# Tables of angles for the state space branch: sums of turns and ScalarE sines in the place of powers by doubling

## The chip, the cores and the metric

The kernel runs on one core of a Trainium2 chip. Its time is the device time of one execution in microseconds (us); the figure compared is the median of several runs. One further execution was taken by the hardware profiler; every row below comes from it.

## What is computed

The reference runs two layers of a hybrid block (Mamba-2, sliding-window and forgetting attention) over 256 tokens of width 1024, then one layer of a second block. That block normalizes the tokens, projects them, and adds three branches: a diagonal state space branch (S5), a sparse attention that keeps 64 keys per query, and attention over a memory. After that comes a mixture of experts, two of 32 per token. The change touches the state space branch alone:

```python
def s5_branch(u, lam_re, lam_im, log_dt, b_re, b_im, c_re, c_im, d_skip, w_glu):
    ...
    lam = lax.complex(lam_re.astype(F32), lam_im.astype(F32))
    dt = jnp.exp(log_dt.astype(F32))[:, None]
    lam_bar = jnp.exp(lam * dt)
    b = lax.complex(b_re.astype(F32), b_im.astype(F32))
    b_bar = ((lam_bar - 1.0) / lam)[..., None] * b
    bu = jnp.einsum('bsgh,gph->bsgp', uf.astype(jnp.complex64), b_bar)
    a = jnp.broadcast_to(lam_bar, (1, seq) + lam_bar.shape)
    _, states = lax.associative_scan(_ssm_combine, (a, bu), axis=1)
    ...
```

There are 32 groups of 64 states, 2048 complex states in all, held as 16 columns of 128 partitions. The recurrence h[n] = lam_bar h[n-1] + bu[n] is turned into two real ones: with lam_bar = rad * e^(i th), the inputs are turned back by n*th, run through a real scan with the factor rad, and turned forward by n*th. For this the kernel needs cos(n*th) and sin(n*th) for n = 0 to 255 and all 16 columns of states: two tables of 128 x 4096 numbers.

## The kernel before

The five engines each run a program of their own, written by hand, and meet at semaphores. A stage is a list of matrix products, each cut into pieces of weights; `weave` and `braid` fix by tables of counts after how many pieces a step of side work comes. Every engine goes through the same list, so the order on an engine never changes at run time, and an engine that waits at one step holds all that stands behind it.

The stages around the change, in the order in which they run:

- `last` of the second layer: TensorE multiplies with weights split in halves (ScalarE casts the high half, `w_hi`, line 2057; VectorE subtracts, `w_lo`, line 1154). Woven in is `prepare` (VectorE from line 1530, ScalarE from 2280): decay `rad` and angle `th` for each state, the rotary angles, and the norm of the memory. In `prepare` VectorE also squares the 16 numbers c5 + i s5 seven times over (`wc`, `ws`), giving the powers 1, 2, 4 ... 128 of e^(i th).
- `kmv`: TensorE projects the memory with whole weights (line 680). Beside it ScalarE and VectorE normalize the tokens (`normalize`), and VectorE then waits for TensorE's transposes and copies them out (`do_split`, the tile `h_all`).
- `table()` on VectorE: the tables for the first 8 columns of states (`R[0]` cosines, `R[2]` sines) by doubling. Entry m+j is entry j times the power m; eight rounds, from 8 x 1 to 8 x 128 columns. GpSimd does the same for the other 8 columns (`R[1]`, `R[3]`), once VectorE is done (`tables_made`) and after the scaling of two quarters of the output matrices (`scale_quarter`, lines 2492 to 2501). VectorE waits for it at unit 4 (`table_made`).
- `u`: TensorE's projection of the branch's inputs, 4 pieces.
- `side`: the 32 steps of `BRAID`. S steps are the state space branch. TensorE's first transposes `uT` and makes `inputs(0)` (line 956); its step for unit u makes `inputs(u+1)`, and for even u from 2 on `outputs` (line 965) before that. VectorE's `unit(u)` turns the inputs, scans them and turns the states, and frees the two PSUM banks of `inputs(u)`, which `inputs(u+1)` takes again. C steps are the sparse attention: its head on VectorE (norm, rotation), transposes, scores (line 917), the search for the 64 highest, then attention. M steps are the memory attention. After each step come 0 to 4 pieces of the projections. The braid begins

```python
BRAID = [("S", 4), ("S", 2), ("S", 2), ("C", 4), ("S", 2), ("C", 0), ("C", 3), ("S", 3), ("C", 3), ("S", 2), ("C", 0), ("C", 1), ("C", 0),
```

so VectorE runs unit 0, unit 1, the head of the sparse attention, unit 2, the first search, unit 3 and so on, in that order.

## Time and profile before

| | |
|---|---|
| median of 3 runs | 2177.31 us (2173.54 to 2178.78) |
| profiled execution | 2178.17 us, of which 2176.3 us are the span between its first and last instruction |
| TensorE matmuls | busy 2006.9 us, 92% of the span |
| VectorE | 1526.8 us, 70% |
| ScalarE | 1117.2 us, 51% |
| GpSimd | 135.6 us, 6% |
| chain that ended last | TensorE 70%, VectorE 20%, ScalarE 5% |

A matmul's busy time overlaps that of its neighbours, so 92% does not mean that TensorE was never kept waiting; the waits are read from its own timeline. Times in the rows are from the start of the span.

### The profile page before, as it was taken

How to read it: one execution, taken by the hardware profiler on the slowest of the kernel's cores; microseconds unless marked ns; L12 is line 12 of the kernel's file. 1: busy time of each engine (PE TensorE's matmuls, PEld its weight loads, DVE VectorE, ACT ScalarE, POOL GpSimd, SP SyncE). 2: the span in 40 equal slices, each digit the busy share in tenths (PEclk: the TensorE clock that was granted, in tenths of full speed). 3: DMA queues.
4: the chain of work that ended last, by engine and by line, in shares of the span. 5: the costliest groups of instructions: out<-in, count | busy, mean ns of one | idle time of the engine just before them, and what ended most of it. 6: DMA issues, size and time to landing. Idle time of an engine off the chain costs nothing.

```text
span 2176.3 us, 25594 instructions
## 1 busy us (share of the span) xinstructions
PE 2006.9 (92%) x9470; PEld 1557.7 (72%) x9470; DVE 1526.8 (70%) x2283; ACT 1117.2 (51%) x1679; POOL 135.6 (6%) x139
## 2 busy tenths in 40 slices
PE   7898999999988899998986889879999999999996
PEld 6777777777877677776543445547888888888885
DVE  5868565555776755557398855338888888888885
ACT  5544554444543555444301022037777777778773
POOL 0000000000000000000074110010000000000000
PEclk9999999999999999999998889989999999999998
DMA  7533434354543444444342322346999999999993
GB/s 227 160 117 117 135 117 136 100 154 147 175 154 88 146 117 126 117 148 153 114 144 83 116 87 97 105 178 236 330 337 329 329 329 324 342 324 330 328 327 136
DMA packets 135325, 411.15 MB, mean 189 GB/s; under 512 B 17789, under 2 KB 19581, under 8 KB 108065
## 3 DMA queue, kind: packets, MB, share of 16 engines
q1 hardware_dynamic: 128912, 407.25, 56.2%
q0 software_dynamic: 6288, 2.26, 0.4%
q8 instruction: 76, 1.25, 0.2%
q14 instruction: 49, 0.39, 0.1%
HBM read 406.23 MB, written 19.47 MB: 196 GB/s over the span
## 4 chain that ended last, share of the span: by engine, by line
PE 70%; DVE 20%; ACT 5%; issue 3%; DMA 1%; SPq 0%; DVEq 0%; ACTq 0%; POOLq 0%
PE bank L632 16%; PE bank L633 16%; PE bank L634 16%; PE bank L680 7%; DVE r L1154 5%; PE bank L1040 3%; DVE w_lo L1154 3%; PE bank L608 2%; PE bank L754 2%; DVE r L1160 1%; ACT w_hi L2057 1%; DVE small L1154 1%; DVE spare L1154 1%; PE bank L803 1%; ACT r L2232 1%
## 5 line engine op out<-in xcount | busy, mean ns | idle before, releaser
L1154 DVE TENSOR_TENSOR w_lo<-w_raw,w_hi 128x1024 fp32r<-128x1024 f32 x372 | 445.3, 1217 | 230.8 <-ACT w_hi L2057 223.3
L2057 ACT CAST w_hi<-w_raw 128x1024 fp32r<-128x1024 f32 x266 | 277.2, 1047 | 166.3 <-PE bank L634 160.0
L632 PE MATMUL bank<-w_hi,h_hi 128*128 128x512 f32 x800 | 329.7, 412 | 18.7 <-DVE w_lo L1154 18.7
L633 PE MATMUL bank<-w_lo,h_hi 128*128 128x512 f32 x800 | 316.7, 396 | 0.0
L634 PE MATMUL bank<-w_hi,h_lo 128*128 128x512 f32 x800 | 316.5, 396 | 0.0
L632 PEld LDWEIGHTS bank<-w_hi,h_hi 128*128 128x128 f32 x800 | 153.5, 192 | 55.7 <-DVE w_lo L1154 13.8
L634 PEld LDWEIGHTS bank<-w_hi,h_lo 128*128 128x128 f32 x800 | 153.1, 191 | 34.2
L633 PEld LDWEIGHTS bank<-w_lo,h_hi 128*128 128x128 f32 x800 | 154.0, 193 | 29.5
L2232 ACT ACTIVATE r<-bank,small 128x256 f32<-128x256 f32 (+1 forms) x152 | 63.8, 424 | 202.4 <-DVE small L1157 202.4
L1154 DVE TENSOR_TENSOR w_lo<-r,w_hi 128x1024 fp32r<-128x1024 f32 x106 | 126.4, 1222 | 30.9 <-ACT w_hi L2342 30.9
L680 PE MATMUL bank<-w_raw,h_all 128*128 128x512 f32 (+1 forms) x320 | 146.1, 613 | 1.1 <-DVE h_all L1154 1.1
L2342 ACT CAST w_hi<-w_raw 128x1024 fp32r<-128x1024 f32 x106 | 109.9, 1056 | 18.7 <-PE bank L634 18.6
L680 PEld LDWEIGHTS bank<-w_raw,h_all 128*128 128x128 f32 x320 | 63.7, 201 | 74.7 <-issue 72.5
L2342 ACT CAST w_hi<-r 128x1024 fp32r<-128x1024 f32 x106 | 109.9, 1060 | 5.2 <-PE bank L634 5.2
L632 PE MATMUL bank<-w_hi,xt_hi 128*128 128x512 f32 x280 | 112.0, 400 | 0.0
L633 PE MATMUL bank<-w_lo,xt_hi 128*128 128x512 f32 x280 | 110.1, 393 | 0.0
L634 PE MATMUL bank<-w_hi,xt_lo 128*128 128x512 f32 x280 | 110.1, 393 | 0.0
L632 PE MATMUL bank<-w_hi,y_hi 128*128 128x512 f32 x256 | 102.9, 402 | 4.9 <-DVE y_lo L1154 3.0
L634 PE MATMUL bank<-w_hi,y_lo 128*128 128x512 f32 x256 | 100.5, 393 | 0.0
L633 PE MATMUL bank<-w_lo,y_hi 128*128 128x512 f32 x256 | 100.5, 393 | 0.0
L1154 DVE TENSOR_TENSOR y_lo<-r,y_hi 128x1024 fp32r<-128x1024 f32 x70 | 84.8, 1224 | 9.3 <-ACT y_hi L2342 8.8
L1438 DVE TENSOR_REDUCE small<-bank 128x2 f32<-128x512 f32 (+1 forms) x76 | 43.8, 576 | 59.1 <-PE bank L928 28.8
(341 smaller groups left out, 4038.7 us busy)
## 6 DMA issues: line engine op xcount, KB each, us to landing
w_raw<-in_w_in SPq DMA_DIRECT2D x236, 512.0 KB, 3.7
r<-in_w_up SPq DMA_DIRECT2D x69, 1024.0 KB, 5.4
w_raw<-in_w_gate SPq DMA_DIRECT2D x68, 1024.0 KB, 5.1
w_raw<-in_w_down SPq DMA_DIRECT2D x36, 1024.0 KB, 5.2
r<-in_w_down SPq DMA_DIRECT2D x34, 1024.0 KB, 5.2
w_raw<-in_w_proj SPq DMA_DIRECT2D x48, 512.0 KB, 3.7
w_raw<-in_w_out SPq DMA_DIRECT2D x24, 512.0 KB, 4.4
w_raw<-in_w_mem_kv SPq DMA_DIRECT2D x8, 512.0 KB, 3.5
```

Source lines behind the costliest of these rows:

```text
L608: done = e.transpose(bank[0:blk.shape[1], j * P:(j + 1) * P], blk, ident)
L632: e.matmul(out_, sh, mh, start=first, stop=False, skip_group_check=shared)
L633: e.matmul(out_, sh, ml, start=False, stop=False, skip_group_check=shared)
L634: return e.matmul(out_, sl, mh, start=False, stop=last, skip_group_check=shared)
L680: done = e.matmul(bank[:, 0:c.n], c.lhs[0][:, kk, t * P:(t + 1) * P], w[:, k, :], start=kk == 0, stop=kk == c.n_k - 1)
L754: done = e.matmul(banks[b][:, c:c + dv], pT[:, (j * kb + kk) * P:(j * kb + kk + 1) * P], v_of(h, kk), start=(kk == 0), stop=(kk == kb - 1))
L1040: done = e.matmul(bank[:, j * 256:(j + 1) * 256], ht[half][:, t, (2 * i + j) * P:(2 * i + j + 1) * P], slots[q % 2][:, t, :, :], start=t = ...
L1154: o.did(v.tensor_tensor(out_, a, b, op), sem, value)
L1438: o.did(v.tensor_reduce(mx, two[:, :, 0:keys_of(t)], AX, MAX))
L2057: a.copy(halves(n)[0], raw_of(n)).then_inc(w_hi, 1)
L2232: a.activation(p_buf[i % 2][:, j * keys:(j + 1) * keys], bank[:, 0:keys], ACT.Exp, bias=mx_all[:, c + j:c + j + 1], accum_out=sum_all[:, c ...
L2342: a.copy(unit_halves(u)[0], unit_raw(u)).then_inc(m_hi, 1)
```

## The change

The 16 columns of states are now cut into two halves of 8 by `table(0)` and `table(1)`, as before, but the entries are no longer products. `turns()` on VectorE expresses the angle as a share of a whole turn (`thn`), takes the whole turns off by adding and subtracting a constant that rounds (`ROUND`), and makes two small tables of 16 numbers for each state: a16 = 0, 16, ... 240 steps and b1 = 0, 1, ... 15 steps. `table(half)` on VectorE adds them, 8 x 16 x 16 = 2048 sums per partition, and takes the whole turns off again. `table(half)` on ScalarE makes the cosine as the sine of a quarter turn less the absolute angle, and the sine. VectorE waits for the first half at unit 0 and for the second at unit 4. The seven squarings in `prepare` go, and GpSimd makes no table; it scales its four quarters one after the other, as their matrices land.

On VectorE `turns()` and `table(0)` stand ahead of `do_split`, `table(1)` behind it. On ScalarE `table(0)` stands behind `kmv`, and `table(1)` between the two evictions of `u`, by `weave(dense(e2["u"]), table(1), n_pieces(e2["u"]), [2], 2)`. The diff without the declarations of semaphores and the removed bodies in full:

```diff
@@ -332,7 +332,7 @@
         ang, sn2, cs2, tmp2, n2 = (stat(64) for _ in range(5))
         sn3, cs3 = tok(sn2), tok(cs2)
         dt5, rad, th, thn, tht, c5, s5, nr, ni, fr5, fi5, den = (stat(ST) for _ in range(12))
-        wc, ws = [c5] + [stat(ST) for _ in range(7)], [s5] + [stat(ST) for _ in range(7)]
+        quarter_turn = stat(1)
         at[0] += -at[0] % 8
         inverse = over_tile("inverse", S, "small", at[0])[0:3, :]
         head_stats, mem_stats = ([stat(T * n) for _ in range(3)] for n in (9, 8))
@@ -1552,13 +1552,6 @@
                     o.prev()
                     tt(dst, dst, den, MUL)
                 o.prev()
-                for j in range(7):
-                    tt(wc[j + 1], wc[j], wc[j], MUL)
-                    tt(tht, ws[j], ws[j], MUL)
-                    o.prev()
-                    tt(wc[j + 1], wc[j + 1], tht, SUB)
-                    stt(ws[j + 1], wc[j], 2.0, ws[j], MUL, MUL)
-                    o.prev()
                 yield
                 v.wait_ge(in_pos, 32)
                 o.did(v.tensor_copy(pos_f[:, :], R[10][:, 0:T + S].bitcast(I32)))
@@ -1577,25 +1570,43 @@
                     tt(memT[:, k:k + 4, t * P:(t + 1) * P], by_k(bank[:, :], 4), bc(small_cols[:, COLS2["g_mem"] + k:COLS2["g_mem"] + k + 4], P), MUL, drained[b], n)
                 yield
 
-            def table():
-
-                ec, es = by_k(R[0][:, :], 8), by_k(R[2][:, :], 8)
-                t1, t2 = (by_k(R[8][:, i * D:(i + 1) * D], 8) for i in range(2))
...
+            def turns():
+
+                first = by_k(R[8][:, 0:512], 2 * ST)
+                whole = by_k(R[8][:, 512:1024], 2 * ST)
+                o.did(v.memset(quarter_turn, HALF_PI))
+                ts(thn, th, TURNS, None, MUL)
+                o.prev()
+                ts(tht, thn, 16.0, ROUND, MUL, ADD)
+                o.prev()
+                ts(tht, tht, ROUND, None, SUB)
+                o.prev()
+                stt(tht, thn, 16.0, tht, MUL, SUB)
+                steps = index_row[:, 0:16].unsqueeze(1).to_broadcast([P, ST, 16])
+                tt(first[:, ST:2 * ST, :], steps, bc(thn, 16), MUL)
+                o.prev()
+                tt(first[:, 0:ST, :], steps, bc(tht, 16), MUL)
+                o.prev()
+                ts(whole, first, ROUND, None, ADD)
+                o.prev()
+                stt(first, whole, ROUND, first, SUB, SUB)
+                o.prev()
+
+            def table(half):
+
+                a16, b1 = (by_k(R[8][:, 0:512], 2 * ST)[:, i * ST + 8 * half:i * ST + 8 * half + 8, :] for i in range(2))
+                turn, whole = (R[i + half][:, :] for i in (2, 0))
+                for i in range(2):
+                    part = slice(4 * i, 4 * i + 4)
+                    tt(turn[:, i * D:(i + 1) * D].rearrange("p (s a b) -> p s a b", s=4, a=16), a16[:, part, :].unsqueeze(3).to_broadcast([P, 4, 16, 16]),
+                       b1[:, part, :].unsqueeze(2).to_broadcast([P, 4, 16, 16]), ADD)
+                o.prev()
+                for i in range(2):
+                    ts(whole[:, i * D:(i + 1) * D], turn[:, i * D:(i + 1) * D], ROUND, None, ADD)
+                o.prev()
+                for i in range(2):
+                    cols = slice(i * D, (i + 1) * D)
+                    stt(turn[:, cols], whole[:, cols], ROUND, turn[:, cols], SUB, SUB, turns_made)
 
             def by_h(a, h):
                 return a.rearrange("p (h c) -> p h c", h=h)
@@ -1719,8 +1730,8 @@
                     ec, es = (a[:, sl, :] for a in angle(k))
                     vre, vim = (by_k(a, 4)[:, sl, :] for a in v_at[k % 2])
                     tm, gr, gi = tmp[:, sl, :], gre[:, sl, :], gim[:, sl, :]
-                    if u == 4:
-                        v.wait_ge(table_made, 1)
+                    if u in (0, 4):
+                        v.wait_ge(table_made, 2 + u // 2)
                     (b0, n0, bank0), (b1, n1, bank1) = await_full(("bu", k, j2, 0)), await_full(("bu", k, j2, 1))
                     bre, bim = by_k(bank0[:, :], 2), by_k(bank1[:, :], 2)
                     o.prev()
@@ -2022,9 +2033,11 @@
             for t in range(T):
                 stt(x3[:, t, :], x3[:, t, :], r[:, t:t + 1], R[9][:, 0:D], MUL, MUL, scaled_made)
             normalize(x3, normed2)
+            turns()
+            table(0)
             run(dense(e2["kmv"]))
             do_split(e2["h"])
-            table()
+            table(1)
             run(dense(e2["u"]))
             braid(dense(e2["side"]), S=ssm(), C=sparse(), M=memory())
             run(dense(e2["memory"]))
@@ -2289,6 +2302,15 @@
                 a.wait_ge(in_mem, 32)
                 rms_factor(mem3, normed)
                 yield
+                yield
+
+            def table(half):
+                sine, cosine = R[2 + half][:, :], R[half][:, :]
+                a.wait_ge(turns_made, 2 * half + 2)
+                a.activation(cosine, sine, ACT.Abs).then_inc(turned_abs, 1)
+                a.wait_ge(turned_abs, half + 1)
+                a.activation(cosine, cosine, ACT.Sin, bias=quarter_turn, scale=-2 * PI).then_inc(table_made, 1)
+                a.activation(sine, sine, ACT.Sin, scale=2 * PI).then_inc(table_made, 1)
                 yield
 
             def sparse():
@@ -2459,8 +2481,9 @@
             a.wait_ge(scaled_made, T)
             rms_factor(x3, normed2)
             run(dense(e2["kmv"]))
+            run(table(0))
             do_split(e2["h"])
-            run(dense(e2["u"]))
+            weave(dense(e2["u"]), table(1), n_pieces(e2["u"]), [2], 2)
             braid(dense(e2["side"]), S=ssm(), C=sparse(), M=memory())
             run(dense(e2["memory"]))
             weave(dense(e2["last"]), bridge(), n_pieces(e2["last"]), BRIDGE)
@@ -2501,33 +2524,9 @@
                 o.did(g.tensor_scalar(c1, c1, -1.0, None, MUL), quarter_scaled)
                 o.prev()
 
-            def table():
-
...
             def ssm():
                 g.wait_ge(bias_used, sum(c.bias is not None for e in L for c in e["forget"] + e["last"]))
-                for k in range(2):
-                    scale_quarter(k)
-                table()
-                for k in range(2, 4):
+                for k in range(4):
                     scale_quarter(k)
 
             def store_rows(x):
```

On VectorE, behind the norm of the tokens and ahead of the copies `h_all` of their transposes, where the rows with + are new (in `small` lie the angles, in the `r` tiles the turns and tables):

```order
 L1157 TENSOR_SCALAR r<-x,small 128x1024 x2
+L1577 MEMSET small 128x1
+L1157 TENSOR_SCALAR small<-small 128x16 x3
+L1160 SCALAR_TENSOR_TENSOR small<-small 128x16
+L1154 TENSOR_TENSOR r<-consts,small 128x256 x2
+L1157 TENSOR_SCALAR r<-r 128x512
+L1160 SCALAR_TENSOR_TENSOR r<-r 128x512
+L1154 TENSOR_TENSOR r<-r 128x1024 x2
+L1157 TENSOR_SCALAR r<-r 128x1024 x2
+L1160 SCALAR_TENSOR_TENSOR r<-r 128x1024 x2
 L1154 TENSOR_TENSOR h_all<-bank,small_cols 128x4x128 x4
```

Nine new rows with 15 instructions now stand between the norm and the copies. On VectorE again, between those copies (`h_all`) and the first operation of unit 0 (`spare_52<-bank,r`), the last rounds of the old table and all of the new one:

```order
-L1154 TENSOR_TENSOR r<-r,small 128x8x128
-L1154 TENSOR_TENSOR r<-r,small 128x1024
-L1154 TENSOR_TENSOR r<-r,small 128x8x128
-L1154 TENSOR_TENSOR r<-r,small 128x1024
-L1154 TENSOR_TENSOR r<-r 128x8x128 x2
+L1154 TENSOR_TENSOR r<-r 128x1024 x2
+L1157 TENSOR_SCALAR r<-r 128x1024 x2
+L1160 SCALAR_TENSOR_TENSOR r<-r 128x1024 x2
 L1154 TENSOR_TENSOR spare_52<-bank,r 128x512
```

The whole doubling, from 128x8 on, is gone from this place, and six instructions of 1024 columns stand there. On ScalarE, from the last evictions of `kmv` (COPY r<-bank) on, through those of `u`, to the copies of `uT` (`spare_51<-bank`) and the evictions of `q2` and `kvi`, before:

```order
L2063 ACTIVATE small<-small 128x2
L2117 COPY r<-bank 128x512 x6
L2172 COPY spare_51<-bank 128x4x128 x2
L2117 COPY r<-bank 128x512 x2
L2117 COPY r<-bank 128x452 x2
L2061 ACT_TABLE_LOAD
L2061 ACTIVATE small<-small 128x18
```

and with the change:

```order
L2130 COPY r<-bank 128x512 x4
L2310 ACTIVATE r<-r 128x2048
L2312 ACT_TABLE_LOAD
L2312 ACTIVATE r<-r,small 128x2048
L2313 ACTIVATE r<-r 128x2048
L2130 COPY r<-bank 128x512
L2310 ACTIVATE r<-r 128x2048
L2312 ACTIVATE r<-r,small 128x2048
L2313 ACTIVATE r<-r 128x2048
L2130 COPY r<-bank 128x512
L2185 COPY spare_51<-bank 128x4x128 x2
L2130 COPY r<-bank 128x512 x2
L2130 COPY r<-bank 128x452 x2
```

The fourth COPY is the last of `kmv`; the two evictions of `u` now have three activations of 2048 columns ahead of each, and one table load is added.

## Rows read from the trace of the kernel before

**Rows 1.** Who waited for whom: TensorE, 1092 to 1500, then 925 to 1062 us (total, times, longest)

```profile
PE bank L956 <- DVE y_all L1154: 35.4, 6, 17.4
...
PE bank L632 <- DVE w_lo L1154: 4.6, 4, 2.7
```

**Rows 2.** Timeline of TensorE (start, length, what, idle before and releaser)

```profile
1092.80 14.00 PE L680 MATMUL bank<-w_raw,h_all 128*128 128x512 f32 x32 [1.13 <-DVE h_all L1154]
...
1109.30 2.00 PE L956 MATMUL bank<-spare,spare_y_lo 128*128 128x256 f32 x8 [0.73 <-ACT spare L2172]
...
1136.84 1.97 PE L956 MATMUL bank<-spare,spare_h_lo 128*128 128x256 f32 x8 [2.98 <-DVE y_all L1154]
1138.64 19.96 PE L680 MATMUL bank<-w_raw,h_all 128*128 128x452 f32 x48
...
1179.50 3.66 PE L956 MATMUL bank<-spare,spare_h_lo 128*128 128x256 f32 x8 [17.44 <-DVE y_all L1154]
...
1272.33 3.75 PE L956 MATMUL bank<-spare,spare_h_lo 128*128 128x256 f32 x8 [3.34 <-DVE y_all L1154]
```

**Rows 3.** Timeline of VectorE, 1070 to 1177 us

```profile
1070.29 2.48 DVE L1160 SCALAR_TENSOR_TENSOR x<-x,small,r 128x1024 f32<-128x1024 f32 x2
...
1080.00 1.42 DVE L1157 TENSOR_SCALAR r<-x,small 128x1024 f32<-128x1024 f32 x2
1090.26 2.48 DVE L1154 TENSOR_TENSOR h_all<-bank,small_cols 128x512 f32<-128x512 f32 x4 [8.84 <-PE bank L608]
...
1119.85 2.36 DVE L1154 TENSOR_TENSOR r<-r 128x1024 f32<-128x1024 f32 x2
...
1149.66 1.03 DVE L1157 TENSOR_SCALAR rows<-rows 128x64 f32<-128x64 f32 x1
...
1159.63 3.82 DVE L1154 TENSOR_TENSOR small<-small 128x18 f32<-128x18 f32 x3
...
1165.93 1.36 DVE L1154 TENSOR_TENSOR r<-r,small 128x1152 f32<-128x1152 f32 x1
...
1176.01 0.69 DVE L1154 TENSOR_TENSOR spare<-bank,r 128x512 f32<-128x512 f32 x1
```

**Rows 4.** Timeline of VectorE, 1241 to 1300 us: unit 4, memory norm

```profile
1241.70 0.69 DVE L1154 TENSOR_TENSOR spare<-bank,r 128x512 f32<-128x512 f32 x1
...
1252.27 0.47 DVE L1160 SCALAR_TENSOR_TENSOR spare<-spare,small_cols,bank 128x256 f32<-128x256 f32 x1
...
1299.05 0.60 DVE L1154 TENSOR_TENSOR small<-small 128x16 f32<-128x16 f32 x3
```

**Rows 5.** Timeline of GpSimd, 1096 to 1166 us

```profile
1096.93 1.13 POOL L2492 TENSOR_TENSOR bias<-spare_y_lo,small 128x512 f32<-128x512 f32 x1 [153.28 <-DMA spare_y_lo<-in_c_im]
...
1163.28 2.37 POOL L2520 TENSOR_TENSOR r<-r 128x1024 f32<-128x1024 f32 x1
```

**Rows 6.** ScalarE: the second eviction of `u`, then two lines (ns min/median/max)

```profile
1106.84 0.58 ACT L2117 COPY r<-bank 128x512 f32<-128x512 f32 x1 [6.28 <-PE bank L680]
...
L2188 ACT ACTIVATE r<-r x4: 1910/1912/1916, 67.2 to 617.3; 128x2048 f32<-128x2048 f32 x4
...
L2276 ACT ACTIVATE small<-small x2: 217/238/258, 980.8 to 992.2; 128x16 f32<-128x16 f32 x1, 128x64 f32<-128x64 f32 x1
L2276 ACT ACT_TABLE_LOAD  x1: 1283/1283/1283, 979.5 to 979.5; - x1
```

**Rows 7.** Timelines of VectorE and TensorE in `last` of the second layer

```profile
983.17 0.90 DVE L1154 TENSOR_TENSOR small<-small 128x16 f32<-128x16 f32 x5
...
987.74 2.36 DVE L1154 TENSOR_TENSOR w_lo<-w_raw,w_hi 128x1024 fp32r<-128x1024 f32 x2
...
1008.09 0.50 PE L632 MATMUL bank<-w_hi,h_hi 128*128 128x512 f32 x1 [2.67 <-DVE w_lo L1154]
...
1008.91 0.63 PE L632 MATMUL bank<-w_hi,h_hi 128*128 128x512 f32 x1
...
1012.30 0.40 PE L634 MATMUL bank<-w_hi,h_lo 128*128 128x512 f32 x1
```

More of the change, by code:

```diff
@@ L246, in build @@
                              "v_ready", "states_ready", "gelu_ready", "y_ssm_done"))
-        tables_made, table_made = sem("tables_made"), sem("table_made")
+        turns_made, turned_abs, table_made = sem("turns_made"), sem("turned_abs"), sem("table_made")
         quarter_scaled, quarter_used, x_final = sem("quarter_scaled"), sem("quarter_used"), sem("x_final")
@@ L1578, in prepare @@
                 yield
-            def table():
-                ec, es = by_k(R[0][:, :], 8), by_k(R[2][:, :], 8)
-                t1, t2 = (by_k(R[8][:, i * D:(i + 1) * D], 8) for i in range(2))
-                o.did(v.memset(ec[:, :, 0:1], 1.0))
-                o.did(v.memset(es[:, :, 0:1], 0.0))
-                o.prev()
-                for j in range(8):
-                    m = 1 << j
-                    c_, s_ = (bc(w[j][:, 0:8], m) for w in (wc, ws))
-                    a_c, a_s, o_c, o_s, ta, tb = ec[:, :, 0:m], es[:, :, 0:m], ec[:, :, m:2 * m], es[:, :, m:2 * m], t1[:, :, 0:m], t2[:, :, 0:m]
-                    tt(o_c, a_c, c_, MUL)
-                    tt(ta, a_s, s_, MUL)
-                    tt(o_s, a_c, s_, MUL)
-                    tt(tb, a_s, c_, MUL)
-                    o.prev()
-                    tt(o_c, o_c, ta, SUB)
-                    tt(o_s, o_s, tb, ADD, tables_made if j == 7 else None)
-                    o.prev()
+            def turns():
[3 more added lines that the diff above has]
+                ts(thn, th, TURNS, None, MUL)
+                o.prev()
+                ts(tht, thn, 16.0, ROUND, MUL, ADD)
[12 more added lines that the diff above has]
+                o.prev()
```

18 lines of the change are left out of this document (removed).

## Prediction

> **What bounds the kernel now.** I first ask where TensorE waits, since it carries 70% of the chain that ended last. Between 1092 and 1500 us its largest single item is 35.4 us in six waits of line 956 (`inputs`) for VectorE to free the banks, the longest 17.4 us [rows 1]. Its timeline shows where: the 17.4 us end at 1179.50, with `inputs(3)` [rows 2]. VectorE's timeline says why. It copies `h_all` until 1092.7, makes its table until 1122.2, and then works without a pause to start the head of the sparse attention at 1149.66 and unit 2 at 1176.01 [rows 3]. So here VectorE is the bound, and its table (29.5 us) is on the path. GpSimd's table begins when VectorE's ends and runs to 1165.65 [rows 5]. While it runs VectorE is slow: three products of 18 columns took 3.82 us at 1159.63 [rows 3], three of 16 columns 0.60 us at 1299.05, with GpSimd idle [rows 4].
>
> The second place is `last` of the second layer. TensorE waits there four times for `w_lo`, 4.6 us in all with 2.67 at 1008.09 [rows 1, 7].
>
> **Part 1, the squarings.** They are 28 instructions of 16 columns. The first two of the five at 983.17 stay, which leaves VectorE free at 983.6, and it went on to `w_lo` at 987.74 [rows 7]: 4.1 us. Behind them come in a row the rotary angles, ScalarE's sines, the norm of the memory and the `w_lo` for which TensorE waits at 1008.09. All of it moves up by 4.1 us. TensorE had 4.6 us of waits to give, so it takes the whole 4.1 and keeps one wait of about 0.5.
>
> After the wait of 2.67 us TensorE ran at its lower level (1.2 GHz): eight matmuls started between 1008.91 (0.63 us busy) and 1012.30 (0.40 again), one every 0.42 us, against half of that at 2.4 GHz [rows 7]. With a wait of 0.5 us I expect no such spell: 1.7 us more. The other end is that the spell stays, 0 us. I take 1.7, since the wait nearly disappears.
>
> The Trainium skill (page "TensorE: Matmul & The Clock Gate", section "What's actually happening") has a monitor with a free-running window set the clock by recent activity, so that whether a wait costs a spell depends also on where it falls. The trace agrees so far: 2.98 us of idleness ahead of 1136.84 cost nothing (8 matmuls in 1.97 us), 3.34 us ahead of 1272.33 doubled them (3.75 us) [rows 2]. By the rule as it stands the sum would lie anywhere between 21.1 and 24.6 us where mine says 22.8.
>
> **Part 2, `turns()` and `table(0)` ahead of `h_all`.** VectorE is free from 1081.4, after the norm, and waited 8.84 us for TensorE's transposes until 1090.26 [rows 3]. New there: a memset and four steps of 16 columns, 0.2 each (0.9); two of 256 columns, between 0.18 and the 0.69 of 512 (0.9); a `tensor_scalar` of 512 (0.45) and a `scalar_tensor_tensor` of 512 (0.7); then per table two additions of 1024 columns (2.36, as `w_lo` in rows 7), two `tensor_scalar` (1.42) and two `scalar_tensor_tensor` (2.48) [rows 3], 6.4 with gaps. Together 9.4 us, ending at 1090.85. So it costs 0.6 us on the path: `h_all` and TensorE's `u` start 0.6 later. The additions read with steps of zero; no row has exactly this pattern, but broadcast products of 1152 columns took 1.36 [rows 3], so I take the plain price. Without the cover of 8.84 us the price would be 9.4.
>
> **Part 3, ScalarE.** An activation of 2048 columns takes 1.91 us, a load 1.28 [rows 6]. The widest sine in the trace has 64 columns: 0.258 us against 0.217 for 16, so 0.85 ns a column and also about 1.9 for 2048. `table(0)` runs from 1090.9 to 1098.0, before TensorE fills the first bank of `u` at 1100.4 (half of the 14.0 us of rows 2). Its eviction ends at 1101.0, `table(1)` takes 5.9 to 1106.9, and the second bank is full at 1107.4 (1106.84 before [rows 6], plus 0.6). Price on the path 0, with only 0.5 us to spare. VectorE's `table(1)` is 6.4 us from 1093.4; GpSimd starts its scaling at 1096.93 [rows 5], so the last four of its instructions may be stretched and it may end between 1099.8 and 1102.9. I take 1101, hidden. The other end costs 1.3 us.
>
> **Part 4, the braid.** The new path from the second eviction on:
>
> - `inputs(0)` at 1109.9, full at 1111.9 (rows 2, plus 0.6). Unit 0 starts there and not at 1122.34. A unit takes 10.6 us when GpSimd is quiet [rows 4]: done at 1122.5, and VectorE waits for the first time.
> - TensorE has four pieces (14.0), then `inputs(1)`, full at 1127.9. Unit 1 runs to 1138.5.
> - The head needs `kvi`: two pieces, `inputs(2)`, two pieces, and an eviction; with 0.39 us a matmul of 452 columns (a little under the 19.96 us for 48 in rows 2, of which 32 have 512) 6.2 + 1.9 + 6.2 + 0.6, so 1142.6.
> - The head took 26.35 us, 10.1 of them after GpSimd had ended (1165.93 to 1176.01 [rows 3]). The 16.3 before that are, undisturbed, two passes over 1152 columns (2.7), the hand-over to ScalarE and back (two activations of 0.22 and a load of 1.28 [rows 6], 1.8) and nine small steps (1.8): 6.3. So 16.4, to 1159.0. This is where GpSimd's missing table pays.
> - Unit 2 frees the banks 3.5 us after its start (1176.01 to 1179.50), at 1162.5. TensorE is there at 1159.6 after `inputs(2)`, six pieces and `outputs(0)`: it still waits, 2.9 us in place of 17.4.
>
> `inputs(3)` moves from 1179.50 to 1162.5: 17.0 us, the 0.6 paid. From here on each side waits for the other as before (search for scores, `inputs(4)` for unit 3), SyncE's loads are released by TensorE's pieces, and the experts start when TensorE is done. So the gain should last to the end; late next is TensorE itself, and ahead of `inputs(4)` to `inputs(6)` VectorE as before. Removing the wait at unit 4 gives nothing, as nobody waited there. The halved clock at `inputs(3)` (3.66 us [rows 2]) I leave, since 2.9 is near the 3.34 that cost it; the other end is 1.8 us better.
>
> **Sum.** 4.1 + 1.7 + 17.0 = 22.8 us. The profiled execution took 2178.17 (span 2176.3), which gives 2155.4; it lies 0.9 above the median of 2177.31, so I say 2155.5.
>
> **Rivals.**
>
> *ScalarE becomes late* (0.15). It has 0.5 us to spare ahead of the transposes `uT`. If VectorE's `table(1)` ends late (1.3) and a wide sine costs a good half more than 1.9, 3 us each, the second eviction of `u` slips by 1.3 + 2.2 - 0.5 = 3.0 and with it all that follows; with sines twice as long by 4.6. Then 2158 to 2160. For it: the small slack. Against: the slope of 0.85 ns.
>
> *The head stays slow* (0.09). If the 26 us are not GpSimd's doing, unit 2 starts 9.9 us later and the gain is 12.9: 2165. Against: the small products of rows 3 and 4, six times as long under GpSimd.
>
> *Slower* (0.04): wide sines on ScalarE are several times dearer than the slope says. Four of them stand ahead of the second eviction of `u`, with 2.9 us of slack in all; the whole gain is gone at (22.8 + 2.9) / 4 = 6.4 us above 1.9, so at 8.3 us each. At 10 us each the kernel takes 2185. For it: no row has a sine wider than 64 columns. The Trainium skill (page "ScalarE: Activation LUTs", section "What ACT_TABLE_LOAD costs") gives every function the same rate per element; no row here shows a wide sine.
>
> *No difference* (0.03): the loads of the experts, and not TensorE, would set the second half, or the change leaves GpSimd's work on the path. Against: its program has no table any more, and SyncE's loads wait for TensorE's pieces.
>
> **Numbers.** My own case has 0.69, with 2152 to 2159 as its range. Down to 2151 lie both clock spells; up to 2166 lie late ScalarE and the slow head. About 0.3% (6.5 us) is what a measurement of this kernel can tell from no change. Faster 0.93, same 0.03, slower 0.04.
>
> **What would show it.** In the new profile: `w_lo` at about 983.7 and no wait above 1 us near 1004; from there all is 5.8 us earlier. `h_all` follows `table(0)` with no wait ended by TensorE. The activations of 2048 columns take 1.9 us, the second eviction of `u` is ended by TensorE. The head of the sparse attention lasts 16 to 17 us. Line 956 waits about 3 us ahead of `inputs(3)`, and the sum of its waits falls from 35.4 to about 18. It would be wrong if the second eviction follows a sine at once and late, if the head keeps 26 us, or if the waits at `inputs(4)` to `inputs(6)` grow by what the first loses.

## The result and the profile after

The changed kernel takes 2153.43 us (median of 4 runs, 2146.2 to 2155.34) against 2176.55 us (2173.54 to 2178.78) of the kernel before: a ratio of 0.989 with a 95% interval of 0.9872 to 0.9909. That is 23.1 us less, and 2 us from the forecast of 2155.5. The profiled execution took 2151.96 us, its span 2150.2.

Of the page, busy times by engine and, from the chain that ended last, the shares by engine:

```profile
PE 2002.1 (93%) x9470; PEld 1556.4 (72%) x9470; DVE 1494.7 (70%) x2226; ACT 1130.6 (53%) x1686; POOL 92.0 (4%) x89
...
PE 75%; DVE 16%; ACT 5%; issue 3%; DMA 1%; SPq 0%; DVEq 0%; ACTq 0%; POOLq 0%
```

TensorE carries 75% of the chain, 70 before, and VectorE 16%, 20 before. GpSimd's busy time fell by 43.6 us and ScalarE's rose by 13.4. The waits of TensorE from 940 to 1500 us (total, times, longest) show the two places of the change; they answer to [rows 1]:

```profile
PE bank L956 <- DVE y_all L1154: 18.1, 4, 7.6
...
PE bank L632 <- DVE w_lo L1154: 1.3, 1, 1.3
```

`inputs` waits half as long, and the `w_lo` waits fell from 4.6 to 1.3 us. The timeline of TensorE in `last` (start, length, what, idle before and its releaser) answers to [rows 7]:

```profile
973.73 0.66 PE L608 MATMUL bank<-consts,r 128*128 128x128 f32 x4 [2.06 <-DVE y_lo L1154]
...
1001.99 0.50 PE L632 MATMUL bank<-w_hi,h_hi 128*128 128x512 f32 x1 [1.33 <-DVE w_lo L1154]
...
1012.35 0.66 PE L608 MATMUL bank<-consts,r 128*128 128x128 f32 x4 [0.59 <-DVE r L1154]
...
1026.68 3.24 PE L608 MATMUL bank<-consts,merged 128*128 128x128 f32 x16 [2.78 <-DVE merged L1154]
```

The row at 973.73 stood at 975.67 before. The change has not acted there yet, so 1.9 us of the difference between the two profiles are not its doing. Counted from this row, the wait for `w_lo` ended 4.16 us earlier and the products at 1012.35 stand 5.78 earlier (1020.07 before). The same engine at the braid, as in [rows 2]:

```profile
1085.31 14.00 PE L680 MATMUL bank<-w_raw,h_all 128*128 128x512 f32 x32 [1.13 <-DVE h_all L1154]
...
1101.81 1.99 PE L956 MATMUL bank<-spare,spare_y_lo 128*128 128x256 f32 x8 [0.73 <-ACT spare L2185]
...
1146.69 3.62 PE L965 MATMUL bank<-spare,spare_y_lo 128*128 128x256 f32 x16
1153.82 3.65 PE L956 MATMUL bank<-spare,spare_h_lo 128*128 128x256 f32 x8 [3.51 <-DVE y_all L1154]
...
1186.17 3.75 PE L956 MATMUL bank<-spare,spare_y_lo 128*128 128x256 f32 x8 [7.57 <-DVE y_all L1154]
```

`u` begins 7.49 us earlier than at 1092.80, and `inputs(3)` at 1153.82 stands 25.7 earlier than at 1179.50. So the stretch between them lost 18.2 us. The wait ahead of `inputs(3)` is 3.51 us in place of 17.44, and its eight matmuls took 3.65 us, as those of `inputs(4)` at 1186.17: both at 1.2 GHz. Ahead of the wait `outputs(0)` (1146.69) had taken 3.62 us for sixteen, and `inputs(0)` at 1101.81 took 1.99 for eight: 2.4 GHz. VectorE in the same stretch, as in [rows 3]:

```profile
1082.77 2.48 DVE L1154 TENSOR_TENSOR h_all<-bank,small_cols 128x512 f32<-128x512 f32 x4
...
1104.03 0.69 DVE L1154 TENSOR_TENSOR spare<-bank,r 128x512 f32<-128x512 f32 x1 [11.94 <-PE bank L956]
...
1119.35 0.69 DVE L1154 TENSOR_TENSOR spare<-bank,r 128x512 f32<-128x512 f32 x1 [4.05 <-PE bank L956]
...
1133.79 1.36 DVE L1154 TENSOR_TENSOR r<-r 128x1152 f32<-128x1152 f32 x1 [3.69 <-ACT r L2130]
...
1139.20 0.60 DVE L1154 TENSOR_TENSOR small<-small 128x18 f32<-128x18 f32 x3
...
1150.33 0.69 DVE L1154 TENSOR_TENSOR spare<-bank,r 128x512 f32<-128x512 f32 x1
```

The copies of `h_all` (four, here at 1082.77) have no idle time ahead of them. Unit 0 waits for its inputs, and so do unit 1 and the head, which waits for ScalarE. The head takes 16.5 us (1133.79 to 1150.33), 26.35 before; its first small operation on `rows`, 0.19 us here and 1.03 before, now stands ahead of the wait and is counted with unit 1. The three small products take 0.60 us, 3.82 before. ScalarE, as in [rows 6]:

```profile
1084.75 1.28 ACT L2312 ACT_TABLE_LOAD   x1
1086.05 2.01 ACT L2312 ACTIVATE r<-r,small 128x2048 f32<-128x2048 f32 x1
...
1096.82 1.89 ACT L2313 ACTIVATE r<-r 128x2048 f32<-128x2048 f32 x1
1099.35 0.58 ACT L2130 COPY r<-bank 128x512 f32<-128x512 f32 x1 [0.64 <-PE bank L680]
```

The second eviction of `u`, at 1099.35, is ended by TensorE, 0.64 us after the last sine. The load took 1.28 us; the wide functions took 1.89 to 2.01.

### The profile page after: what moved, and what is told of

Same layout as the page of the kernel before. It is cut to its first block, busy times and chain, and to the rows that moved or that the text cites. A ratio compares the mean times of both kernels' runs of the same rounds, so it can differ in the third digit from the quotient of the medians.

```text
span 2150.2 us, 25494 instructions
## 1 busy us (share of the span) xinstructions
PE 2002.1 (93%) x9470; PEld 1556.4 (72%) x9470; DVE 1494.7 (70%) x2226; ACT 1130.6 (53%) x1686; POOL 92.0 (4%) x89
## 4 chain that ended last, share of the span: by engine, by line
PE 75%; DVE 16%; ACT 5%; issue 3%; DMA 1%; SPq 0%; DVEq 0%; ACTq 0%; POOLq 0%
PE bank L632 17%; PE bank L634 17%; PE bank L633 17%; PE bank L680 9%; DVE r L1154 4%; PE bank L1040 3%; DVE w_lo L1154 3%; PE bank L608 2%; PE bank L754 2%; DVE r L1160 1%; ACT w_hi L2070 1%; PE bank L956 1%; ACT r L2245 1%; PE bank L803 1%; PE bank L737 1%
## 5 line engine op out<-in xcount | busy, mean ns | idle before, releaser
L1154 DVE TENSOR_TENSOR h_lo<-w_raw,h_hi 128x1024 fp32r<-128x1024 f32 x70 | 83.6, 1215 | 0.0
```

The lines of the kernel that those rows point to most:

```text
L1154: o.did(v.tensor_tensor(out_, a, b, op), sem, value)
```

## What the braid's 18.2 us are made of

Both profiles give this sum by VectorE's rows, each counted from the start of `u`, because all else in the two is then in step. Unit 0 starts 18.72 us after it, 29.54 before (the table): 10.8 us. Units 0 and 1 are busy 22.0 us from the start of unit 0 to the head, waits left out, 27.3 before: 5.3. The head takes 9.8 less. But VectorE now waits 4.05 + 3.69 = 7.7 us in between, where it never waited before. So unit 2 starts 10.8 + 5.3 + 9.8 - 7.7 = 18.2 us earlier, 65.02 us after `u` in place of 83.21. That the terms add up proves nothing, since they are the pieces of one interval; the sum only says which pieces became shorter.

This is still one profile against another. The runs change the terms one at a time. Each states the time from the start of `u` to the start of the 32 matmuls with `y_all` that follow, called the braid here: 295.14 us before (1092.80 to 1387.94), 276.90 after (1085.31 to 1362.21). Its end in the kernel before, then in the changed one:

```profile
1387.94 14.00 PE L680 MATMUL bank<-w_raw,y_all 128*128 128x512 f32 x32 [0.78 <-ACT y_all L2094]
```

```profile
1362.21 14.00 PE L680 MATMUL bank<-w_raw,y_all 128*128 128x512 f32 x32 [0.78 <-ACT y_all L2107]
```

What stands behind it took 788.4 and 788.0 us. In the profiles of all fourteen kernels of this document it took 783.8 to 788.4, though no edit touches it, so the length of the braid is a better measure of an edit than the total time.

## The experiments

### The squarings put back

```diff
+ wc, ws = [c5] + [stat(ST) for _ in range(7)], [s5] + [stat(ST) for _ in range(7)]
...
+ for j in range(7):
+     tt(wc[j + 1], wc[j], wc[j], MUL)
...
```

The 28 small instructions stand in `prepare` again; nobody reads them.

> The changed kernel with the seven squarings put back into `prepare`, where nothing uses their results. The output stays the same. My theory: they sit on a chain VectorE - ScalarE - VectorE that ends at TensorE's wait for `w_lo` in `last` of the second layer. TensorE's waits there go from 1.3 back to about 4.6 us, the one near 1002 us back to 2.7, followed by a spell of some 3.4 us at the lower clock: 5.8 us more, about 2159 us. Rival: the stage has slack for 4 us of small VectorE work, and the profile's difference there was between two runs: at most 1 us more, 2154.

Measured: 2156.15 us (2150.83 to 2157.1), ratio 0.9894 (0.9877 to 0.9911). The interval overlaps that of the changed kernel, so by the time alone neither theory is chosen. The timeline of TensorE chooses (lines are one further down in this kernel):

```profile
975.93 0.66 PE L609 MATMUL bank<-consts,r 128*128 128x128 f32 x4 [2.06 <-DVE y_lo L1155]
...
1008.38 0.50 PE L633 MATMUL bank<-w_hi,h_hi 128*128 128x512 f32 x1 [2.67 <-DVE w_lo L1155]
...
1020.36 0.66 PE L609 MATMUL bank<-consts,r 128*128 128x128 f32 x4 [0.59 <-DVE r L1155]
```

The wait of 2.67 us is back. From the first of these rows to the last it is 44.43 us, as before the change (44.40), and 38.62 in the changed kernel. Behind the wait the granted clock (fourth column, of full speed) from 1010 to 1015 us was

```profile
1010.00:1015.00 5.00, 5.00 (x18) 0.73 0.58 193
```

where it is 1.00 in the changed kernel. The squarings alone cost 5.8 us there: 4.2 of waiting and 1.6 of matmuls at 1.2 GHz behind it. The braid took 277.8 us, 0.9 more than after, so they matter little elsewhere. The medians show only 2.7 of these 6.7 us. In the profile the stretch behind the braid took 784.2 us, 3.8 less than in the changed kernel, and it has nothing to do with the squarings; so the price of 5.8 is shown by the rows and not by the time.

### GpSimd kept busy

```diff
-                for k in range(4):
+                for k in range(2):
                     scale_quarter(k)
+                for _ in range(30):
+                    o.did(g.tensor_tensor(bias_rows[0][:, :], bias_rows[1][:, :], bias_rows[1][:, :], SUB))
+                    o.prev()
+                for k in range(2, 4):
+                    scale_quarter(k)
```

Thirty subtractions of 512 columns on GpSimd, beside units 0 and 1 and the head. Their result is dead.

> The changed kernel, with 30 subtractions of 512 columns on GpSimd between its second and third scaling. They write to a tile that nobody reads and nobody waits for them, so they can act by their company alone. My theory: VectorE is slowed while GpSimd works. Unit 1 takes some 5 us longer, of which 3.7 vanish in VectorE's wait for `kvi`, and the head of the sparse attention goes from 16.5 to about 26 us. `inputs(3)` is 10 to 11 us later: about 2164 us. Rival: VectorE was slow there for a reason of its own and only the late start of unit 0 counted: the head keeps 16.5 us, no change, 2153.

Measured: 2162.97 us (2161.46 to 2164.8), ratio 0.9931 (0.9914 to 0.9947), 9.5 us more than the changed kernel. GpSimd's row, then VectorE's:

```profile
1110.58 41.76 POOL L2532 TENSOR_TENSOR bias<-bias 128x512 f32<-128x512 f32 x30
```

```profile
1125.53 0.69 DVE L1154 TENSOR_TENSOR spare<-bank,r 128x512 f32<-128x512 f32 x1
...
1126.85 1.11 DVE L1154 TENSOR_TENSOR spare<-spare,y_all 128x512 f32<-128x512 f32 x1
...
1130.56 5.55 DVE L1750 TENSOR_TENSOR_SCAN spare<-small,spare 128x256 f32<-128x256 f32 x4
...
1144.64 1.02 DVE L1157 TENSOR_SCALAR rows<-rows 128x64 f32<-128x64 f32 x1
...
1163.55 0.69 DVE L1154 TENSOR_TENSOR spare<-bank,r 128x512 f32<-128x512 f32 x1
```

The four scans of a unit take 5.55 us in place of 2.44, and a unit takes 19.1 in place of 10.6. The head, whose end GpSimd no longer covers, takes 18.9. By the same sum: VectorE's work from unit 0 to the head is 16.3 us longer, the 7.7 us of waits are used up, the head is 2.4 us longer: 11.0. Unit 2 started 10.9 us later. The braid took 287.6 us, 10.7 more. The forecast of the time held, but I had looked for the price in the head (26 us expected, 18.9 measured) and most of it came from the units. So this run shows that GpSimd's company costs VectorE time, and not yet that it made the old head 26 us long; the old kernel in another order shows that below. Beside GpSimd's table these had lost only 5.3 us; its first products took 0.21 us each, the subtractions here 1.4.

One detail shows what GpSimd slows. The product at 1126.85 reads two tiles in SBUF and took 1.11 us; later ones took 1.4. The one at 1125.53 reads a PSUM bank and a tile, and took 0.69, the undisturbed time. That agrees with a rule of the Trainium skill (page "SBUF — State Buffer", section "Who interferes with whom"): a VectorE instruction with two SBUF inputs contends with a GpSimd instruction that reads SBUF. It is not the only case here: the `tensor_scalar` at 1144.64 has one tile as its input and took 1.02 us, where it takes 0.19 in the changed kernel.

### VectorE late, in two doses

```diff
             table(1)
+            for _ in range(18):
+                o.prev()
+                tt(R[8][:, 0:D], R[8][:, D:2 * D], R[8][:, D:2 * D], MAX)
             run(dense(e2["u"]))
```

Eighteen dead operations of 1024 columns behind `table(1)`.

> The changed kernel with 18 operations of 1024 columns on VectorE (some 22 us, on a tile that is free) behind `table(1)`, so that unit 0 starts as late as with the old table, about 10.4 us later than now, with GpSimd idle. My theory: VectorE's two new waits ahead of unit 1 (4.05) and ahead of the head (3.7) take up 7.7 us, and 2.7 us reach TensorE at `inputs(3)`: about 2156 us. Rival: VectorE's 22 us were the path, and the late start is carried through: 10 us more, 2164.

Measured: 2166.79 us (2163.16 to 2167.24), ratio 0.9945 (0.9929 to 0.9962). VectorE's timeline (lines beyond the edit are three further down):

```profile
1094.58 32.10 DVE L1154 TENSOR_TENSOR r<-r 128x1024 f32<-128x1024 f32 x18
...
1149.80 1.36 DVE L1154 TENSOR_TENSOR r<-r 128x1152 f32<-128x1152 f32 x1 [1.44 <-ACT r L2133]
...
1166.34 0.69 DVE L1154 TENSOR_TENSOR spare<-bank,r 128x512 f32<-128x512 f32 x1
```

The dose was wrong: GpSimd scales the output matrices at the same time, so the eighteen took 32.1 us, where I had reckoned with 22. Unit 0 started 20.3 us late. The wait of 4.05 us ahead of unit 1 was gone, and 1.44 us were left of the one ahead of the head. So 6.3 us were absorbed, which leaves 20.3 - 6.3 = 14.0 us for unit 2, and it was 13.6 late. The braid took 16.3 us more. Neither expectation fits the time, so the dose was cut to ten:

> Ten operations of 1024 columns on VectorE whose results nobody reads, behind table(1): a smaller dose than the eighteen of the earlier run, which took 32.1 us beside GpSimd's scaling and made unit 0 late by 20.4 us. Ten should take about 17.8 us, of which the idle time ahead of unit 0 (11.9 us in the changed kernel) takes 11.9: unit 0 starts about 6 us late. Theory (between unit 0 and the head VectorE waits 4.05 us for the inputs of unit 1 and 3.69 us for ScalarE's squares, 7.7 us in all, and that much lateness costs nothing): the head ends at most 1 us late, 2153 to 2156 us. Rival (each microsecond by which unit 0 is late is paid at the inputs of unit 3): 2159 to 2161 us.

```profile
1092.20 19.84 DVE L1154 TENSOR_TENSOR r<-r 128x1024 f32<-128x1024 f32 x10
...
1135.91 1.36 DVE L1154 TENSOR_TENSOR r<-r 128x1152 f32<-128x1152 f32 x1 [1.44 <-ACT r L2133]
```

The ten took 19.84 us, unit 0 was 8.1 us late, and unit 2 was 2.1 us late (its scan at 1156.56, 1154.43 in the changed kernel). The time was 2151.24 us (2144.31 to 2153.21), ratio 0.9885 (0.9866 to 0.9904): not more than without them. So six microseconds of lateness were absorbed in VectorE's waits, as the theory has it. The other 2.1 reached TensorE, whose `inputs(3)` stand 2.05 us later behind `u`, and still the braid was 3.5 us shorter, 273.4, in this profile, which is of the fastest of the four executions (2144.31 us). The view by stretches of 25 us (length, TensorE busy, matmuls, granted clock, DMA share, GB/s), first of the changed kernel, then of this one:

```profile
1160.00:1185.00 25.00, 17.80 (x59) 0.92 0.41 127
...
1210.00:1235.00 25.00, 19.13 (x57) 0.86 0.29 85
1235.00:1260.00 25.00, 21.66 (x73) 0.80 0.22 67
```

```profile
1160.00:1185.00 25.00, 19.93 (x63) 0.98 0.40 126
...
1210.00:1235.00 25.00, 19.10 (x66) 0.95 0.29 85
1235.00:1260.00 25.00, 20.68 (x90) 0.98 0.32 106
```

The granted clock was 0.92, 0.86 and 0.80 in three stretches in which it is 0.98, 0.95 and 0.98 here; from 1260 to 1285 it is the other way, 0.86 there and 0.80 here. The waits at line 956 were a little longer (19.5 us in five). The eight matmuls of `inputs(5)` took 1.97 us here behind a wait of 3.69, and 3.75 us in the changed kernel behind one of 3.67. So which waits are followed by a spell at 1.2 GHz differs between two executions with nearly the same waits. Between `inputs(3)`, 2.05 us late, and the end of the braid, 3.5 early, this profile gained 5.6 us, of which the waits of `inputs(4)` to `inputs(6)` are 0.4. Why a spell comes in one and not in the other stays open.

### Both together

> The edits of the two kernels before together: the late start of unit 0 and GpSimd's 30 operations. My theory: the costs are not additive, since there is only one slack of 7.7 us for both. Late by 10.4, unit 1 slowed by 5 and the head by 10, less 7.7: about 18 us more, 2171. Rival: they add up to the sum of the two runs alone, 11 + 3 = 14 us, 2167.

Measured: 2182.71 us (2181.58 to 2185.2, 10 runs), ratio 1.0023 (1.0013 to 1.0032). VectorE from unit 0 to unit 2:

```profile
1130.62 0.69 DVE L1154 TENSOR_TENSOR spare<-bank,r 128x512 f32<-128x512 f32 x1
...
1166.87 1.35 DVE L1154 TENSOR_TENSOR r<-r 128x1152 f32<-128x1152 f32 x1
...
1183.42 0.69 DVE L1154 TENSOR_TENSOR spare<-bank,r 128x512 f32<-128x512 f32 x1
```

The head follows unit 1 at once. The braid took 307.7 us, 30.8 more than after, where the two alone cost 10.7 and 16.3, together 27.0. The slack is there once: each alone had used 7.7 and 6.3 us of the same waits. Both expectations had reckoned with smaller doses and lie 12 and 16 us below the measured time, and the test is not a clean one: the eighteen operations made unit 0 late by 3.6 us more than alone, and GpSimd, which now ended at 1164.25, slowed the units by 14.2 us and the head not at all. By VectorE's rows unit 0 is 23.9 us late, the units take 14.2 us more, and 7.7 of waits are gone: 30.4. The two obstacles together, in these larger doses, take back more than the change had gained.

### The tables behind the copies of `h`

```diff
-            turns()
-            table(0)
             run(dense(e2["kmv"]))
             do_split(e2["h"])
+            turns()
+            table(0)
             table(1)
```

> The turns and both halves of the table stand behind the copies of h on VectorE, where the old powers stood; nothing is left out. What VectorE has to do is the same, only its order changes: it starts the turns some 10 us later than in the changed kernel, h is copied when the mean square is known, and table(1) ends about where it ended before (it was last in both orders). My theory (the copies of h have no price for standing behind the turns as long as their matmuls aren't done; ScalarE takes its work in order, so that its three wide functions of table(0), which stand ahead of both evictions of u, now begin about 10 us later and hold the second eviction of u with them): the wait behind the second eviction passes from TensorE to ScalarE, the transposes of u, the inputs of units 0 to 3 and with them the head come some 8 to 10 us later; about 6 of that is paid at the inputs of unit 3: 2158 to 2164 us. Rival (VectorE had 11.9 us of idle time ahead of unit 0, which takes the late table; the order is free): 2153 to 2155 us, no wait of TensorE for a bank of u.

Measured: 2167.55 us (2165.8 to 2170.17), ratio 0.9958 (0.9942 to 0.9974): 14.1 us more than the changed kernel. Only VectorE's order was changed; on ScalarE `table(0)` still stands ahead of the evictions of `u`. ScalarE's timeline and TensorE's:

```profile
1097.12 1.91 ACT L2310 ACTIVATE r<-r 128x2048 f32<-128x2048 f32 x1 [14.33 <-DVE r L1160]
...
1111.37 1.89 ACT L2313 ACTIVATE r<-r 128x2048 f32<-128x2048 f32 x1
1113.17 0.56 ACT L2130 COPY r<-bank 128x512 f32<-128x512 f32 x1
```

```profile
1113.79 1.97 PE L608 MATMUL bank<-consts,r 128*128 128x128 f32 x8 [14.61 <-ACT r L2130]
```

ScalarE starts `table(0)` at 1097.12, 14.3 us later. The second eviction of `u` stands behind both halves and has no idle time before it. TensorE waits 14.6 us for it. The direction was that of the theory, the size was not. I had expected 6 us to be paid, because VectorE's slack would take the rest. But it is TensorE itself that stands still, ahead of its own work, and no slack of VectorE gives that back: the braid took 290.8 us, 13.9 more. So 14 of the change's 23 us hang on the place of VectorE's `turns()` and `table(0)` ahead of `do_split`, with ScalarE's order as it is. Its other order was not tried.

### Another order of the braid

The sum shows what is left: VectorE waits for one strand where the other has work. Five orders were tried, and one of them on the kernel before as well. None leaves anything out.

```diff
-BRAID = [("S", 4), ("S", 2), ("S", 2), ("C", 4), ("S", 2), ("C", 0), ("C", 3), ("S", 3), ("C", 3), ("S", 2), ("C", 0), ...
+BRAID = [("S", 4), ("S", 2), ("S", 2), ("S", 2), ("C", 4), ("S", 0), ("C", 0), ("C", 5), ("S", 2), ("C", 4), ("C", 0), ...
```

> The changed kernel with another order of the braid, nothing left out: unit 2 of the state space ahead of the head of the sparse attention, unit 3 between the head and the first search, unit 4 between the two searches. Theory (after the change VectorE is idle ahead of unit 1, the head and both searches, 4.05, 3.69, 6.76 and 5.11 us, each time for one operand of the other strand, and TensorE waits 18.1 us in all at the state space's inputs; the strands only have to be laid so that each fills the other's gaps): the sum of TensorE's waits at the inputs falls by 5 to 12 us, 2142 to 2149 us. Rival (TensorE gives its own work in the braid in the same order, and what one wait loses another takes on, since VectorE with its 190 us of work bounds the stretch): 2152 to 2156 us.

Measured: 2134.99 us (2133.78 to 2136.13), ratio 0.9808 (0.9791 to 0.9826), better than expected. TensorE's waits at `inputs` fell from 18.1 to 8.6 us, and the braid from 276.9 to 263.1. Less halved clock may make up part of the rest: the granted clock from 1085 to 1335 is 0.95, where it was 0.92. With unit 2 alone moved (`("S", 2), ("C", 4), ("C", 0), ("S", 3)` from the fourth entry on):

> The changed kernel with only unit 2 moved ahead of the head, all else in its old order, nothing left out. Theory: the head waits 3.69 us for ScalarE today; with unit 2 (10.8 us) ahead of it this wait is gone, and the bank of the inputs of unit 3 is free earlier, so that TensorE's 3.51 us wait at them is gone too; but the scores of the head come 7 us later for the search: 2149 to 2153 us. Rival (unit 2's inputs are computed behind the head's work on TensorE, VectorE waits for them, and the head with all searches comes later by the same time): 2154 to 2162 us.

Measured: 2140.92 us (2137.97 to 2144.26), ratio 0.983 (0.9811 to 0.9849); TensorE waits 13.8 us at `inputs`. The gain is larger than expected here too, and the rival, that the head's delay eats it, fell. The first order on the kernel before:

> The kernel before with the braid's order of v2_units_ahead and nothing else changed: the powers by doubling stay, half of them on GpSimd, as do the squarings. It asks how much of the 41 us between the kernel before and v2_units_ahead needs the change. Theory (what the change frees is the start of the braid on VectorE, 15.3 us earlier counted from the copies of h, and 9.8 us of the head's stretch on VectorE beside GpSimd; the order hides waits that exist in either kernel; but the slack that the new order uses up was then no longer there to hide the late start, and three units now run beside GpSimd's powers, so that the change is worth at least its 23 us here too): 2152 to 2162 us. Rival (the two gains are the same microseconds: with units first, the late start and the slow head are covered by TensorE's own work): 2136 to 2146 us.

Measured: 2163.86 us (2161.63 to 2164.82), ratio 0.9939 (0.9922 to 0.9956). TensorE's waits from 960 to 1300 us, then the head and the start of unit 3 on VectorE:

```profile
PE bank L956 <- DVE y_all L1154: 19.4, 4, 12.1
```

```profile
1170.95 0.19 DVE L1157 TENSOR_SCALAR rows<-rows 128x64 f32<-128x64 f32 x1
...
1187.59 0.69 DVE L1154 TENSOR_TENSOR spare<-bank,r 128x512 f32<-128x512 f32 x1
```

In this kernel GpSimd still makes its table, which ends at 1166.7, and the head stands behind that: it takes 16.6 us. Unit 2 now stands beside GpSimd's widest products and takes 20.4 us (1150.12 to 1170.56) in place of 10.6; its four scans take 9.44. So the 26.35 us of the head in the kernel before were GpSimd's doing, and not the head's own.

This lies 2 us past the range of the theory, and 18 past the rival's. The order gives 12.7 us without the change and 18.4 with it; put the other way, the change is worth 28.9 us in this order and 23.1 in the old one. The braids alone, 284.1 us here, give less of a difference: 21.0 for the change in this order and 18.2 in the old one, 11.0 for the order without the change and 13.8 with it. The longest wait, 12.1 us, is still the one for a VectorE that starts late and has GpSimd beside it. Two more steps, unit 5 one step earlier, then units 5 and 6:

> The order of v2_units_ahead with unit 5 one step earlier (behind the first part of the attention, not the third), nothing left out. In v2_units_ahead VectorE waits 1.19, 3.07 and 6.21 us for TensorE ahead of three maxima before unit 5, and TensorE then waits 3.34 us for unit 5. Theory (unit 5 fills these gaps, TensorE's wait vanishes, one level of its clock with it): 2128 to 2133 us. Rival (the first of the waits hold until the scores are there, whatever stands between, and unit 5 now delays the maxima for which ScalarE and TensorE wait): 2135 to 2141 us.

> As v5_unit5_early, and unit 6 one step earlier too (behind the head of the memory, not two parts of attention later), nothing left out. Theory: another 1 to 4 us less than v5_unit5_early, since VectorE's waits of 4.21 and 2.33 us ahead of two maxima are filled. Rival: the bank of unit 6's inputs is not there yet, and VectorE waits for it instead: 1 to 5 us more than v5_unit5_early.

Measured: 2132.63 us (2129.13 to 2133.8), ratio 0.9796 (0.9777 to 0.9814), and 2134.54 us (2131.61 to 2138.11), ratio 0.9803 (0.9786 to 0.9821). Neither can be told from the other or from the first order by its interval. For unit 5 the time lies in the range of the theory, but its mechanism failed: TensorE's wait ahead of `inputs(6)` did not vanish, it grew from 3.34 to 5.21 us. With unit 6 early too, TensorE waits 3.38 us ahead of `inputs(7)`, where it did not wait before, and the gain that the theory named did not come. Last, two pieces of TensorE's dense work moved from ahead of unit 1's inputs to behind the head, `("S", 2)` and `("C", 6)` for the `("S", 4)` and `("C", 4)`, in the order with unit 5 early:

> As v5_unit5_early, but two pieces of TensorE's dense work (8 matmuls of 452 or 512 columns each) that stood ahead of unit 1's inputs stand behind the head instead, nothing left out. Theory (in v5_unit5_early VectorE waits 3.89 us for the inputs of unit 1, and 4.74 us in the head; with the inputs one unit earlier by about two pieces, 3.5 to 8 us, the three units ahead of the head run without a gap, and the dense work that is moved fills the place where TensorE waits 5.25 us for them at the inputs of unit 3): 2126 to 2131 us. Rival (the head starts when its own operands from the dense projections are evicted, and these come no earlier; what VectorE gains it waits for there): 2131 to 2136 us.

Measured: 2129.13 us (2123.7 to 2132.02), ratio 0.9785 (0.9772 to 0.9799), 47 us less than the kernel before and the lowest of all; its interval and that of the order with unit 5 early still overlap. Its waits at `inputs` from 1080 to 1300 us, and VectorE's rows with idle time from the copies of `h_all` to the start of the head:

```profile
PE bank L956 <- DVE y_all L1154: 4.6, 1, 4.6
```

```profile
1104.04 0.69 DVE L1154 TENSOR_TENSOR spare<-bank,r 128x512 f32<-128x512 f32 x1 [11.94 <-PE bank L956]
...
1138.99 1.36 DVE L1154 TENSOR_TENSOR r<-r 128x1152 f32<-128x1152 f32 x1 [1.61 <-ACT r L2130]
```

The braid took 252.2 us, 24.7 less than in the changed kernel; the profile is of the fastest of the five executions, 5.4 us below their median. Between 1085 and 1210 us TensorE's granted clock is 1.00 throughout.

## Why the prediction was right

*Part 1, the squarings.* `w_lo` starts 4.2 us earlier and the spell behind the wait is gone: 5.8 us forecast, 5.78 read and 5.8 in the run with the squarings alone. The remaining wait is 1.33 us, not 0.5, so my limit of 1 us was missed. TensorE arrives there 2.8 us earlier, where my 0.5 needs 1.9: the three small waits were 1.9 us together, and the other 0.9 are 0.3 for each. I put them down to the first product behind a wait, which overlaps no other (0.50 us, where one follows another every 0.23); no run tests that.

*Part 2, the cover.* `turns()` and `table(0)` took 8.9 us, not 9.4. The copies of `h_all` follow at 1082.77, which is 109.04 us behind the row at 973.73. In the run with the tables behind them they were released by TensorE 109.05 us behind the same row. So nothing was paid of the 0.6 that I charged: VectorE and TensorE are ready together. The run with the tables behind the copies shows what the cover is worth, and that I had named the wrong price for losing it: I wrote 9.4 us, and it is 14, since ScalarE stands behind VectorE, and TensorE behind ScalarE.

*Part 3, ScalarE.* Wide sines take 1.89 and 2.01 us, 1.9 was forecast from the slope of two narrow ones. The slack at the second eviction was 0.64 us, forecast 0.5. So the rival of a late ScalarE and that of dear sines both fall. The trace agrees with the rate that the Trainium skill gives for every function (page "ScalarE: Activation LUTs", section "What ACT_TABLE_LOAD costs"). VectorE's `table(1)` ended at 1092.1, which is 1099.6 in the time of the profile before; I had 1101. Only its last pair was stretched by GpSimd (3.21 us, 2.36 undisturbed). It was hidden in either case.

*Part 4, the braid.* 18.2 us measured, 17.0 forecast. Of the 1.2 between them 0.6 are the price of part 2, which was not paid, and 0.7 come from the head, which started 48.5 us after `u` (forecast 49.2); 0.1 went back in the head, which took 16.5 us (16.4). That a quiet GpSimd makes the head short is shown twice: by the changed kernel, and by the old one in the new order (16.6 us). So the rival of the slow head falls too. `inputs(3)` waits 3.51 us (2.9), still at 1.2 GHz afterwards (3.65 us for 8 matmuls), and the sum of the waits is 18.1 (18). The waits ahead of `inputs(4)` to `inputs(6)` were 7.14, 3.68 and 3.34 us before and are 7.57, 3.67 and 3.34 now: 14.2 and 14.6, so they did not take on what the first lost. The two small ones ahead of `inputs(1)` and `inputs(2)`, 0.80 and 2.98 us before, are gone.

*The sum.* 5.8 + 18.2 = 24.0. 0.2 us went back ahead of `kmv`: behind the wait of 2.78 us at 1026.68 sixteen transposes took 3.24 us, where before the change they ended 2.79 us behind the same wait (at 1034.40 in the profile before). The granted clock from 1030 to 1035 was 0.56. The 1.9 us ahead of the change and 0.4 behind the braid make it the 26.1 us between the two spans. Between the medians it is 23.1, for 22.8 from the sum. How the 1.9 us arise stays open: kernels whose program is the same up to there reach this row at 973.6 to 974.3 in some profiles and at 975.7 to 976.7 in others. Such a shift moves medians as well, and so do the 4.6 us by which the stretch behind the braid differs. So that the total came within 2 us of the forecast is in part luck; the steps above are compared from row to row and free of both.

*The clock.* The sum rested on one spell going and one staying, and both did in the profile. That the one at `inputs(3)` stayed was not sure: in the runs with the squarings back and with ten dead operations the same wait of 3.5 us was followed by 2.58 and 2.48 us for the eight matmuls, not 3.65. The bounds of 21.1 and 24.6 us that I gave by the rule of the Trainium skill hold the measured 24.0 without deciding between the two readings. The runs agree with what I drew from the Trainium skill (page "TensorE: Matmul & The Clock Gate", section "What's actually happening"), that recent activity sets the clock and a wait alone does not decide: the same wait of 2.78 us was once followed by the full rate and once by 1.2 GHz.

## What to carry to other kernels

When two engines alternate on one path, add up the waits that will appear on the engine that is bound: what it saves beyond them is the gain, what it loses within them is free, and this slack can be spent once. A removed stage leaves new waits behind, and they say how the order should be laid now: here another order was worth 18 to 24 us more, 12.7 without the change. When work is moved to an in-order engine, look first at what stands behind it there: here the same work cost nothing ahead of the copies and 14 us behind them.

## What the runs showed beyond that

- VectorE and GpSimd slow each other. Beside GpSimd products of 512 columns VectorE's products of 512 columns with both inputs in SBUF went from 0.69 to as much as 1.5 us, four scans from 2.44 to 5.55 (9.44 beside products of 1024 columns), operations of 1024 columns from about 1.2 to 2.0; products with one input in PSUM stayed at 0.69. GpSimd's own products went from 1.04 to as much as 2.05.
- A wait of TensorE costs more than the idle time ahead of its row, by about 0.3 us each in `last`.
- Ten dead operations on VectorE, 19.8 us of work, left the kernel no slower: most fell into waits, and the difference in TensorE's spells was larger than the rest (braid 273.4 us with them, 276.9 without, one profile each).
- TensorE waits of 2.78 us were followed by either level of its clock; those of 3.3 to 3.7 in the braid mostly by 1.2 GHz, but 1.97 us for eight matmuls occurred as well, behind 3.69 and behind 3.35 us, in the run with ten dead operations.
